# Reordering three stretches of a hybrid encoder layer: the norm in front of the input projection, the entry of the recurrence, and the loads of the next sequence's x

## What is computed

```python
h = rms_norm(x, norm_mix_pre)
proj = h @ w_in                                   # q, k, v, z, x/B/C, dt
attn = rms_norm(neighbourhood_attention(q, k, v, rpb))
xbc = silu(depthwise_conv(xbc))
y = ssd_scan(forward) + ssd_scan(backward) + xs * d_skip
y = rms_norm(y * silu(z))
x = x + rms_norm(concat(attn, y) @ w_out)
h = rms_norm(x, norm_ffn_pre)
return x + rms_norm((gelu(conv(h @ w_gate)) * (h @ w_up)) @ w_down)
```

## Time and profile before

| what | value |
|---|---|
| median of three runs | 2894.7 us (2892.27 to 2896.05) |
| profiled execution | 2891.83 us |
| its span, first to last instruction | 2890.1 us |
| mean granted clock of TensorE in it | 0.992 |
| PE busy | 2788.5 us (96%) |
| DVE, ACT, POOL busy | 69%, 44%, 21% |

### The profile page before, as it was taken

How to read it: one execution, slowest core, us unless ns; L and a number is a source line. 1 busy time by engine, 2 the same in 40 slices (tenths; PEclk the granted TensorE clock), 3 DMA queues, 4 the chain that set the end, 5 groups by cost and what they waited for, 6 DMA issues and landing times.

```text
span 2890.1 us, 36492 instructions
## 1 busy us (share of the span) xinstructions
PE 2788.5 (96%) x12752; PEld 2211.6 (77%) x12752; DVE 2007.6 (69%) x3125; ACT 1284.4 (44%) x2557; POOL 592.9 (21%) x845
## 2 busy tenths in 40 slices
PE   7999999899999999999999999998999999999997
PEld 5778787568777778888778787875677788888875
DVE  3657755784789987775647577458767777778656
ACT  4324555355643333345543255553666333333444
POOL 4622222560014430000100322226500000000001
PEclk9999999999999999999999999998999999999999
DMA  7551232314545541243532412332335222114243
GB/s 226 142 149 54 68 101 90 112 54 160 172 149 179 188 143 59 76 165 117 194 105 71 131 60 75 118 106 70 113 126 191 71 88 81 59 59 160 92 134 129
DMA packets 151253, 334.83 MB, mean 116 GB/s; under 512 B 22353, under 2 KB 25073, under 8 KB 151072
## 3 DMA queue, kind: packets, MB, share of 16 engines
q1 hardware_dynamic: 114864, 206.73, 22.6%
q0 software_dynamic: 36208, 125.77, 13.2%
HBM read 264.51 MB, written 69.90 MB: 116 GB/s over the span
## 4 chain that ended last, share of the span: by engine, by line
PE 77%; DVE 12%; ACT 4%; issue 4%; DMA 2%; POOL 1%; SPq 0%; DVEq 0%; ACTq 0%; POOLq 0%
PE A L1121 5%; PE A L1122 4%; PE A L1123 4%; PE G L1121 4%; PE G L1122 4%; PE G L1123 4%; PE G L668 4%; PE A L1173 4%; PE A L1175 4%; PE A L1174 4%; PE G L669 4%; PE G L670 4%; PE G L698 3%; PE G L699 3%; PE G L700 3%
## 5 line engine op out<-in xcount | busy, mean ns | idle before, releaser
L1765 DVE TENSOR_TENSOR wlo<-raw,whi 128x512 fp32r<-128x512 f32 x626 | 440.7, 710 | 472.7 <-ACT whi L1246 471.1
L1246 ACT CAST whi<-raw 128x512 fp32r<-128x512 f32 x630 | 383.1, 619 | 444.2 <-PE A L1175 147.3
L668 PE MATMUL G<-arena_rounded,whi 128*128 128x512 f32 x768 | 317.9, 414 | 6.7 <-DVE wlo L1765 3.9
L670 PE MATMUL G<-arena_rounded,wlo 128*128 128x512 f32 x768 | 303.7, 395 | 0.0
L669 PE MATMUL G<-arena_rounded,whi 128*128 128x512 f32 x768 | 303.5, 395 | 0.0
L1121 PE MATMUL A<-arena_rounded,whi 128*128 128x512 f32 x560 | 221.8, 396 | 0.5 <-DVE wlo L1765 0.4
L1121 PE MATMUL G<-arena_rounded,whi 128*128 128x512 f32 x560 | 222.0, 396 | 0.3
L1122 PE MATMUL A<-arena_rounded,whi 128*128 128x512 f32 x560 | 221.5, 395 | 0.0
L1123 PE MATMUL A<-arena_rounded,wlo 128*128 128x512 f32 x560 | 221.5, 395 | 0.0
L1123 PE MATMUL G<-arena_rounded,wlo 128*128 128x512 f32 x560 | 221.5, 395 | 0.0
L1122 PE MATMUL G<-arena_rounded,whi 128*128 128x512 f32 x560 | 221.5, 395 | 0.0
(11 more groups left out here) (363 smaller groups left out, 6168.4 us busy)
## 6 DMA issues: line engine op xcount, KB each, us to landing
raw<-w_gu_tiles SPq DMA_DIRECT2D x184, 256.0 KB, 3.4
raw<-w_out_rows SPq DMA_DIRECT2D x144, 256.0 KB, 2.9
raw<-w_tok_tiles SPq DMA_DIRECT2D x96, 256.0 KB, 2.7
raw<-w_in_tiles SPq DMA_DIRECT2D x92, 256.0 KB, 2.8
raw<-sums_of_down SPq DMA_DIRECT2D x88, 256.0 KB, 2.6
raw<-w_down_rows SPq DMA_DIRECT2D x66, 256.0 KB, 3.2
f_by_chunk<-small POOLq DMA_DIRECT2D x24, 512.0 KB, 4.6
arena<-w_down_rows POOLq DMA_DIRECT2D x22, 512.0 KB, 6.5
```

Of the source, the lines that this page charges most:

```text
L668: nc.tensor.matmul(out, whi[:, u % SPLIT_SLOTS, w], hi, start=first, stop=False)
L670: return nc.tensor.matmul(out, wlo[:, u % SPLIT_SLOTS, w], hi, start=False, stop=last)
L1246: nc.scalar.copy(whi[:, u % SPLIT_SLOTS, w], weights_of(u)).then_inc(S["hi_split"], 1)
L1765: tt(wlo[:, u % SPLIT_SLOTS, w], weights_of(u), whi[:, u % SPLIT_SLOTS, w].bitcast(F), ALU.subtract).then_inc(S["lo_split"], 1)
```

## The change

- SP loads tiles 0 to 3 of sequence 0's x, then job 1's two weight units, waits until tile 1 has landed, and only then loads tiles 4 to 7.
- For tiles 0 to 3 of sequence 0, ACT takes the root after each tile, and DVE inverts and scales each tile by itself. An additional root on one column stands at ACT's start.
- In both halves and both sequences PE turns four channel blocks at first; the other four are turned inside the first product's loop, block k + 4 ahead of the product of block k (`norm_and_turn`).
- In the recurrence chunk 0's exponents lie in p0 and p1 as those of all chunks, and the state that comes from behind for chunk 0 lies in p2. `back_state(6)` comes ahead of `spread`. DVE adds up the last backward state first, its 8 multiplications of the attention stand between the steps of chunk 0, and the three splits stand behind them.
- Five of the eight places in `X_LOADED` are one or two units later (57 to 59 and 60 to 62 by two).

```diff
-X_LOADED = (37, 41, 57, 60, 45, 63, 66, 69)
+X_LOADED = (38, 41, 59, 62, 45, 64, 67, 70)
...
         def ef_pair(c):
-            return p0 if c else p2
+            return p0
         def eb_pair(c):
-            return p1 if c else p3
+            return p1
...
                     load(0)
-                    load_x(0)
-                for job in range(1 if s == 0 else 0, J_OUT):
+                    load_x(0, range(4))
+                    load(1)
+                    sp.wait_ge(S["x_in1"], 16)
+                    load_x(0, range(4, TT))
+                for job in range(2 if s == 0 else 0, J_OUT):
...
+                def norm_and_turn(half):
+                    def ready(k):
+                        pe.wait_ge(S["norm_applied"], nth("norm_applied", 8 * half + k + 1))
+                        if k + 4 < KD:
+                            turned(0, half, x_block, (k + 4,))
+                    return ready
...
-                turned(0, 0, x_block)
+                turned(0, 0, x_block, range(4))
...
-                gemm(0, (0, 1), h_hi, h_lo, after_norm(0))
+                gemm(0, (0, 1), h_hi, h_lo, norm_and_turn(0))
                 gemm(1, (2, 3), h_hi, h_lo)
                 pe.wait_ge(S["x_scaled"], nth("x_scaled", 8))
-                turned(0, 1, x_block)
-                gemm(2, (0, 1), h_hi, h_lo, after_norm(8))
+                turned(0, 1, x_block, range(4))
+                gemm(2, (0, 1), h_hi, h_lo, norm_and_turn(1))
...  (exponents, d == 0, g == 0)
                             elif c == 0:
-                                pe.wait_ge(S["cb_out"], nth("cb_out", 1))
-                                pe.wait_ge(S["xv_out"], nth("xv_out", TT))
+                                pe.wait_ge(S["b_read"], nth("b_read", 7))
+                            elif c == 1:
+                                pe.wait_ge(S["picked"], nth("picked", 2))
...  (exponents, d == 1, g == 0)
-                            elif c == 0:
-                                pe.wait_ge(S["xa_out"], nth("xa_out", 2 * TT))
-                                pe.wait_ge(S["am_full"], nth("am_full", 8))
-                            elif c > 1:
+                            elif c:
                                 pe.wait_ge(S["m_ready"], nth("m_ready", 2 * c))
...  (within, c == 0)
-                            pe.wait_ge(S["ef_exp"], nth("ef_exp", 2))
+                            pe.wait_ge(S["yib_out"], nth("yib_out", 1))
...
                 back_state(5)
+                back_state(6)
                 spread(0)
                 spread(1)
-                back_state(6)
                 exponents(0, 0)
-                pe.wait_ge(S["b_read"], nth("b_read", 7))
-                incoming(0, SB, p0, "yib_done")
+                pe.wait_ge(S["xa_out"], nth("xa_out", 2 * TT))
+                pe.wait_ge(S["xv_out"], nth("xv_out", TT))
+                pe.wait_ge(S["cb_out"], nth("cb_out", 1))
+                incoming(0, SB, p2, "yib_done")
                 exponents(0, 1)
...  (ahead of inner(1, ...))
-                            pe.wait_ge(S["m_ready"], nth("m_ready", 2))
+                            pe.wait_ge(S["am_full"], nth("am_full", 8))
...  (ACT, at its start)
+            nc.scalar.activation(srt[:, 0:1], epsc[:, :], ACT.Sqrt)
...  (front_stats)
-                    if i % 4 == 3:
+                    if q == 0 and i < 4:
+                        nc.scalar.activation(stat[:, 0, i:i + 1], stat[:, 0, i:i + 1], ACT.Sqrt, bias=epsc[:, :], scale=1.0 / D
+                                             ).then_inc(S["x_rt"], 1)
+                    elif i % 4 == 3:
...  (front_scale)
                     for i in range(4 * half, 4 * half + 4):
+                        if not q and not half:
+                            dve.wait_ge(S["x_rt"], i + 1)
+                            inverse(stat[:, 0, i:i + 1])
                         ts(x_tile(i), x_tile(i), stat[:, 0, i:i + 1], None, ALU.mult).then_inc(S["x_scaled"], 1)
...  (DVE, entry of the recurrence)
                 back_sum(5)
-                att_scaled(0)
-                att_scaled(1)
                 back_sum(6)
-                split_to(UNITS_TO[J_OUT] + 3)
+                att_scaled(0, (0, 1))
                 pick(0, 0)
+                att_scaled(0, (2,))
                 from_behind(0)
                 masses(0, 0)
+                att_scaled(0, (3,))
+                att_scaled(1, (0,))
                 pick(0, 1)
+                att_scaled(1, (1, 2))
                 masses(0, 1)
+                att_scaled(1, (3,))
+                split_to(UNITS_TO[J_OUT] + 3)
```

More of the change, by code:

```diff
@@ L190 @@
        "un_done": TT, "v_in0": 16 * PAIRS, "v_in1": 16 * PAIRS, "v_in2": 16 * PAIRS, "v_in3": 16 * PAIRS, "v_out": TT, "v_saved": 128, "weights_used": UNITS_W,
-       "x1_ready": TT, "x1_rt": TT, "x1_saved": 16 * TT, "x_rt": 2, "x_scaled": TT, "xa_out": 2 * TT,
+       "x1_ready": TT, "x1_rt": TT, "x1_saved": 16 * TT, "x_rt": 5, "x_scaled": TT, "xa_out": 2 * TT,
        "xt_done": N_FRONT + N_FFN, "xtok_done": 3 * TT, "xv_out": TT, "xw_ready": 14, "y_saved": 16 * TT, "yb_ready": TT,
@@ L722, in after_norm, with turned @@
                     return lambda k: pe.wait_ge(S["norm_applied"], nth("norm_applied", n + k + 1))
-                def turned(first, half, tile):
-                    for k in range(KD):
+                def turned(first, half, tile, ks):
+                    for k in ks:
                         n = 8 * half + k
@@ L1792, in front_scale @@
                 def front_scale(q, half):
-                    dve.wait_ge(S["x_rt"], q * PER["x_rt"] + half + 1)
-                    inverse(stat[:, 0, 4 * half:4 * half + 4])
+                    if q or half:
+                        dve.wait_ge(S["x_rt"], q * PER["x_rt"] + (half + 1 if q else 5))
+                        inverse(stat[:, 0, 4 * half:4 * half + 4])
                     for i in range(4 * half, 4 * half + 4):
+                        if not q and not half:
+                            dve.wait_ge(S["x_rt"], i + 1)
+                            inverse(stat[:, 0, i:i + 1])
                         ts(x_tile(i), x_tile(i), stat[:, 0, i:i + 1], None, ALU.mult).then_inc(S["x_scaled"], 1)
@@ L2040, in from_behind @@
                     at = arena[:, SB + c, :]
-                    tt(heads(at), heads(spans(p0)), per_head(ECS[1], c), ALU.mult).then_inc(S["yib_out"], 1)
+                    tt(heads(at), heads(spans(p0 if c else p2)), per_head(ECS[1], c), ALU.mult).then_inc(S["yib_out"], 1)
                 def from_ahead(c):
@@ L2085, in y_lo, with att_scaled @@
                         m.then_inc(S["ml_done"], 1)
-                def att_scaled(half):
+                def att_scaled(half, ks):
                     dve.wait_ge(S["rs_done"], nth("rs_done", half + 1))
-                    for k in range(4):
+                    for k in ks:
                         stt(att(k, half), att(k, half), col("attn", k), A[:, 3 - half, :], ALU.mult, ALU.mult).then_inc(S["am_full"], 1)
```

## The result

The changed kernel takes 2877.6 us (median of six runs, 2875.7 to 2880.4) against 2894.6 us of the kernel before, measured beside it (six runs, 2890.9 to 2897.6). The ratio is 0.9943, with a 95% interval of 0.993 to 0.9956: 16.9 us faster. The profiled execution took 2877.0 us with a span of 2875.3, 14.8 us less than the span before.

What follows compares the result with a forecast made beforehand. The prediction took PE, busy 96% of the span, as the bound, so edits pay only where PE waits. Terms -1.5 - 0.75 + 6.0 + 3.0 - 14.8 - 5.2 = -13.2 from 2894.7 gave 2881.5 us, range 2874 to 2890.5.

Steps and rivals of the forecast that it cites:

- Start, first half of sequence 0: Front of sequence 0: earlier table load and scalings start PE 3.3 us earlier, but waiting for unit 3's split leaves -1.5 us.
- First half of sequence 1: Front of sequence 1: products fill the gaps between four transpositions, -0.75 us; the 1.62 us pause ahead of block 4 stays.
- Second half: Both fronts: transposes of blocks 12 to 15 now stand behind the wait for unit 4's split, +3.0 us per sequence, +6.0.
- The clock: Half rate behind the fronts' new gaps: one fall for the 3.65 us gap, one for both 2.8 us gaps, +3.0 us.
- The recurrence: Recurrence entry: DVE's multiplications fill its waits, 15.3 us instead of 22.76; -7.4 per sequence, -14.8 (-6.5 each with slower splits).
- x later: Down projection: x loaded two units later near n = 57 to 62 removes waits for splits, -5.2 us, bounds -3.4 and -5.4.
- half rate in the recurrence: Rival: PE's pauses of nearly 2 us in the recurrence keep the clock at half rate, 2889.4 us; chance 0.14.
- The second half isn't late: Rival: in the fronts unit 4's split on DVE comes ahead of the turned blocks' rests, about 2873 us; chance 0.10.
- x still stalls: Rival: in the down projection transfers, not their place, set the 5.4 us, so no gain there, 2886.7 us; chance 0.08.
- POOL did not take over: Rival denied here: POOL's chain of scalings and additions sets the recurrence loop, the 14.8 us go, 2896.3 us; chance 0.06.
- The new gaps did not keep PE slow: Rival denied here: half rate lasts 17 us after each of three new front gaps, 8.5 us each, 2904 us; chance 0.04.

Runs made afterwards that it cites:

- the last experiment: The changed kernel with SP's first loads in the order of the kernel before (weights 0, all eight tiles of x, then weights 1 and on): 2884.7 us in one run.
- the runs on the start: The changed kernel without the dummy square root ahead of tile 0, 2881.3 us; the changed kernel with SP's first loads in the old order, 2884.7 us.
- the fifth and sixth kernels: The changed kernel with splits of units 4 and 5 ahead of blocks 8 to 15, 2866.5 us; then also unit 3's ahead of tiles 4 to 7's norm, 2861.3 us.

## Why the prediction was right, and where it was off

The time of 2877.6 lies within the range of 2874 to 2890.5, 3.9 us below the forecast of 2881.5, and the direction is the forecast's. Of the 3.9 us, some 2.1 are the difference between the medians (16.9 us apart) and the two profiled executions (spans 14.8 apart), which the terms can't show; 0.9 are errors of the terms, 0.7 are stretches that no term had, and 0.1 is the median of the kernel before. The terms themselves come out so near in part by luck: x gained 2.0 us more than forecast, and the clock cost 1.6 us more. Term by term:

- **Start, first half of sequence 0: -1.5, measured -1.65.** The gap ahead of unit 3 is 3.64 us against 3.65 forecast. The chain was read rightly: the gain at PE's start is spent on waiting for unit 3's split. Two steps were right without their reasons. Job 1's weights ahead of tiles 4 to 7 are no free move but what makes ACT's blocks start early at all, as the last experiment shows. And the added roots didn't lie in waits for tiles 1 to 3: ACT has no such wait in the changed kernel, from tile 0's square at 8.82 to the last root at 14.11. Tile 0 came 0.82 us later than before (8.82 against 8.00), and tile 3 was there without a wait; that the first transpose came at 15.64, near the 15.9 forecast, is the balance of the two. The Trainium skill, "ScalarE: Activation LUTs" (What ACT_TABLE_LOAD costs), would have the switch cost about 2.66 us; no trace here bears it out, since without the early root the square root starts 1.29 us after the load does, at 10.73.
- **First half of sequence 1: -0.75, measured -0.5.** Transposes of blocks 0 to 3 to those of 8 to 11 took 17.18 us before and 16.70 after.
- **Second half: +3.0 each, right.** The gap behind block 11 is 2.83 us in both sequences (forecast 2.8). In the run without the early root no fall of the clock came behind it in sequence 0, so the bare length can be read: 38.94 to 49.90, T + 10.96 for unit 5's first product (T is the first transpose of block 8), where the prediction had T + 10.95.

```profile
38.94 1.91 PE L735 MATMUL A<-ident,arena 128*128 128x128 f32 x16
43.67 0.66 PE L735 MATMUL A<-ident,arena 128*128 128x128 f32 x4 [2.83 <-DVE wlo L1781]
...
49.90 0.50 PE L671 MATMUL G<-arena_rounded,whi 128*128 128x512 f32 x1 [1.46 <-DVE wlo L1781]
```

- **The clock: +3.0, measured +4.6, just beyond the upper bound of 4.5.** The first gap's fall cost 1.54 us (unit 3 to block 8: 4.44 us instead of 2.90), the other two 1.61 and 1.42 (12.57 and 12.38 us against 10.96). Forecast was one fall for these two together, between the row with 2.59 us of idle time and no fall behind it and that with 3.26 and one. Sequence 0's gap is 2.83 us in all six kernels that have it, and from its end to unit 5's first product it is 7.82 or 7.83 us in four of them and 6.22 or 6.23 in two (the runs on the start): the same gap costs a fall of 1.6 us or none. In sequence 1 it cost 1.4 to 1.6 us in four of the six, nothing in the run with the front alone, and 2.8 us in the run with the multiplications in a row. So one fall for each gap is what came most often, and the forecast of one for two was too low; what decides between them stays open.
- **The recurrence: -14.8, measured -15.3.** The stretch is 15.25 us against 15.3, the splits took 1.89 against 1.90 in the place without POOL's instruction, and DVE has no pause. Of the two bounds the right one was taken; that POOL's instruction was the cause of the longer splits was not tried by itself. The trace of the kernel before speaks for it: all 24 of DVE's 128x512 splits that took more than 0.75 us ran beside a POOL instruction, among them the first of these three (1.72 us); but most of those beside one took no longer than the others.
- **x later: -5.2, measured -7.2, beyond the bound of -5.4.** The mechanism was right, and the term mis-sized. The 5.4 us are five waits of PE, and a wait costs more than its idle column says. Six rows of the kernel before show it:

```profile
1390.32 0.40 PE L1175 MATMUL A<-whi,arena_rounded 128*128 128x512 f32 x1
1391.83 0.50 PE L1173 MATMUL A<-whi,arena_rounded 128*128 128x512 f32 x1 [1.11 <-DVE wlo L1765]
1392.16 0.39 PE L1174 MATMUL A<-wlo,arena_rounded 128*128 128x512 f32 x1
...
1394.49 0.39 PE L1175 MATMUL A<-whi,arena_rounded 128*128 128x512 f32 x1
1394.87 0.50 PE L1173 MATMUL A<-whi,arena_rounded 128*128 128x512 f32 x1
1395.21 0.39 PE L1174 MATMUL A<-wlo,arena_rounded 128*128 128x512 f32 x1
```

A matmul starts every 0.233 us here, but a row is 0.39 to 0.50 us long, since it ends with its result. From 1390.32 to 1392.16 are 1.84 us for two slots of 0.233: 1.37 us are lost, not 1.11. Five waits at 0.27 more each make 5.4 + 1.4 = 6.8 of the 7.2 us. The rest is two shorter waits that the idle column doesn't show at all, since the row before had not ended: at 1394.87 a product starts 0.38 us behind the matmul before it, and the next 0.34 us later, which loses 0.25 us, and at 2821.93 another loses 0.23. Start to start, the seven waits come to 3.65 us in sequence 0 and 3.55 in sequence 1, which is what the two places gained.

- **What no term had: -0.7 in sum.** Before, the profile had a stall of 3.26 us and a fall at 781. In the profiles of the changed kernel and of all ten experiments PE waits 1.0 to 2.4 us there and the place is 1.5 to 3.7 us shorter, also where only x or only the front was changed and everything around the place is as before. So it isn't the change's doing; why that one profile of before had the long stall stays open. Against it stand half rate ahead of the recurrence (+1.6) and at its end (+0.9, +1.2). These come and go between executions, as below.

Of the rivals, half rate in the recurrence didn't come in the changed kernel: the windows of the changed kernel show the clock at 1.00 through PE's pauses of 2.06 and 1.65 us, and lower only behind them, when DVE's stretch was nearly over.

```profile
537.00:541.00 4.00, 1.95 (x12) 1.00 0.00 0
541.00:545.00 4.00, 2.27 (x15) 1.00 0.35 98
545.00:549.00 4.00, 4.00 (x10) 0.57 0.10 33
```

The Trainium skill, "TensorE: Matmul & The Clock Gate" (Part 1), says that idleness returns the array to 1.2 GHz, and the trace agrees behind the gap of 3.64 us (0.69 over 32 to 36); in the recurrence the level fell only once the pauses were over. With the multiplications in a row, where PE's waits were 3.43 and 1.57 us, half rate did come there, and 0.8 to 1.0 us more were lost behind the pick. "The second half isn't late" was refuted by the gaps, and its premise, a split ahead of the turned blocks, is what the fifth and sixth kernels built: 11 and 16 us better than the change. "x still stalls" fell with no wait left. POOL did not take over: from chunk 1's first pick to chunk 2's it took 11.71 us (546.94 to 558.65), and 11.72 before. The new gaps did not keep PE slow for 15 us, but for some 3 us each. The 17 us on which that rival was built are not one stretch either: between the two windows of the earlier trace rows the clock had come back in part, 0.67 over 536 to 540 and 0.76 over 540 to 544.

## What to carry to other kernels

Where work is put between the products of a loop, look at what its results are queued with on the engines that write them: here the transposes were harmless, and the splits that stood behind other work on ACT and DVE cost the loss; with three of them moved ahead the kernel is 16 us faster still. A stall in front of a pipelined engine is best priced by start-to-start times around it, less the slots of the instructions in between, not by its idle column. A sum of steps followed engine by engine held to some tenths of a us for four of six terms; what remained were the waits for x, priced by the idle column, and the clock, which differs between executions, so that one profile of before can't show it.

## What the runs showed of the hardware that was not expected

- Half rate comes at the same few places in some executions and not in others, with the same code there. At the transposes ahead of the recurrence (about 518 us, 1946 in sequence 1) it took 1.6 us in the changed kernel, 3.3 with only x moved (and 1.5 more at 497), 1.7 and 3.3 with only the front, and nothing in the profile of before; ten transposes took 2.38 us there in the changed kernel and 1.29 before. At the end of the recurrence it took 0.9 to 1.2 us in some: over 628 to 636 the clock was 0.61 in the changed kernel and 1.00 in the kernel before. A few such falls together are of the size of the spread between runs of one kernel (2888.4 to 2898.7 us for the kernel before, over its 30 runs), and the mean granted clock goes with that spread: 0.991 to 0.993 in five runs under 2891 us, 0.989 or 0.990 in four over 2898.
- At the start the first sixteen transposes took 3.65 us in the run with x loaded at once, 0.228 each, and sixteen took 1.91 us at 37.84 in the changed kernel, 0.119 each. So the first ones ran at about half the rate, while the granted clock of their windows reads 1.00.
- The first four tiles of x land at times that vary by almost a us between runs: the first transpose of the seven kernels with the new start lay between 15.08 and 15.92, that of the three with the old start between 18.52 and 19.62.
